# Low halves of stationary weights placed 128 bytes further in their buffer

## The chip, the core and the metric

One core of a Trainium2 chip runs the whole program. The metric is the device time of one execution in microseconds, median of three. In the rows below PE is TensorE's matmuls, PEld its loads of the stationary operand, DVE is VectorE, ACT is ScalarE, POOL is GpSimd, SP the engine that issues the DMAs.

## What is computed

Three transformer layers on 256 tokens of width 1024, in float32: a layer of retention and latent attention, a layer of block attention (MoBA), and a layer of banded attention and a state-space mixer, followed by a feed-forward block of width 4096. Most of the work is products of the activations with large weight matrices:

```
h = x @ w_in                       # per layer, several thousand columns
y = concat([ret_out, mla_out]) @ w_out
h = h + jnp.square(jax.nn.relu(hn @ w_ff1)) @ w_ff2
```

## The kernel before

Every weight matrix comes from HBM in pieces of up to 512 rows by 512 columns, which land in one of three slots of `raw`. ScalarE copies a piece, rounded, into `w_hi` (lines 768 and 778). VectorE, or now and then GpSimd, subtracts that from `raw` and writes the remainder to `w_lo` (line 798). The activations have been split in the same way. A product then takes three matmuls, high by high, high by low and low by high, which add up in PSUM.

There are two layouts. In "tok" chunks (rows of the result are tokens) an activation tile of 128x128 is stationary and 512 columns of weights are moving (lines 1069 to 1071; 1121 to 1123 are a few with 256 moving columns at the end of the program). In "feat" chunks (rows of the result are features) a weight tile of 128x128 is stationary and 256 columns of activations, 1024 bytes on each partition, are moving. Their inner step is this, for each of the four tiles of 128 features in a piece and each 128 rows of weights:

```
pe.matmul(o, wh[k][:, fs], hi[:, ka, :], ...)    # line 1077
pe.matmul(o, wh[k][:, fs], lo[:, ka, :], ...)    # line 1078
ins = pe.matmul(o, wl[k][:, fs], hi[:, ka, :], ...)    # line 1079
```

The stationary tile is loaded anew for each of the three, so that the order of loads is high, high, low, 512 bytes each on every partition. While one matmul runs, the load for the next one runs beside it.

`w_hi` and `w_lo` have two homes each, and a home has two halves of `HALF` = 1024 elements with `SLACK` = 128 elements of spare room behind each. `place(p, e)` turns an element's number in a piece into its place in the buffer. It adds the spare room for the second half, and `p.shift`, which is 80 elements (320 bytes) for pieces of feat chunks and 0 for all others. In the built program the starts of both buffers, of all homes and halves, and of all activation tiles are multiples of 512 bytes. So a feat tile of either part begins 320 bytes past a multiple of 512 bytes, and a moving tile begins on one.

The order of work on each engine is written out by `plan`, and nothing in it depends on `place`. Waits are counted in pieces and half pieces.

Of the kernel before, what the change touches and what calls it, by code (L numbers as in the profile page):

```python
# [7 lines left out]
F32 = mybir.dt.float32  # L8
# [45 lines left out]
HALF = 1024  # L54
SLACK = 128
# [58 lines left out]
class Piece:  # L114


    def __init__(self, chunk, src, nk, k0, cols, order=None, rows=0):
        self.chunk, self.src, self.nk, self.k0, self.cols = chunk, src, nk, k0, cols
        self.order = order
        self.raw = nk * (rows or cols)  # L120
        self.size = nk * cols
        self.turn_after = None
        self.split = False
        self.by_tokens = False
        self.room = 2 * self.size if order == "beside" else self.size
        self.off = 0
        self.shift = 0
        self.home = None
        self.full = nk == 4
        self.ahead_of = None  # L130
# [387 lines left out]
def build(nc, w, out):  # L518
    chunks, pieces, steps = plan(w)
    order = {}  # L520
    for s in steps:
        p = s[1] if s[0] == "piece" else s[1][0] if s[0] in ("part", "rows_of", "tokens") else None
# [17 lines left out]
    for s in steps:  # L540
        if s[0] == "epi":
            c = s[1]
# [4 lines left out]
    with ExitStack() as ctx:  # L547
        def sb(name, shape, dt=F32):
            return ctx.enter_context(nc.sbuf_tensor(name, shape, dt))
# [7 lines left out]
        w_hi = sb("w_hi", [P, 2, 2 * (HALF + SLACK)], F32R)  # L557
# [30 lines left out]
        acc = ctx.enter_context(nc.psum_tensor("acc", [P, 4, 2, 512], F32))  # L588
# [80 lines left out]
                p.home = p.n % 2  # L669

        for p in pieces:
            p.shift = 80 if p.chunk.layout == "feat" else 0

        def room_of(p):

            if p.home == "R3":
                return v_hi[:, :], v_lo[:, :]
            if p.home == "R1":
                return b_hi[:, :], b_lo[:, :]
            return w_hi[:, p.home, :], w_lo[:, p.home, :]  # L680

        def place(p, e):

            if p.home in (0, 1):
                return p.off + e + (p.off + e) // HALF * SLACK + p.shift
            return p.off + e

        def weights_of(p):

            def tiles(b):  # L690
                return [b[:, place(p, k * p.cols):place(p, k * p.cols) + p.cols] for k in range(p.nk)]
            return [tiles(b) for b in room_of(p)]

        def split_views(p, k0, k1):

            r = raw[:, p.slot, k0 * p.raw // p.nk:k1 * p.raw // p.nk]
            at = place(p, k0 * p.cols)
            parts = [b[:, at:at + (k1 - k0) * p.cols] for b in room_of(p)]  # L700
            if p.order == "pairs":
                return [(r.rearrange("p (k f t) -> p k t f", t=2, f=P),
                         *[v.rearrange("p (k t f) -> p k t f", t=2, f=P) for v in parts])]
            if p.order == "beside":
                both = room_of(p)[0][:, at:at + 2 * p.size].rearrange("p (k c n) -> p k c n", k=p.nk, c=2)
                return [(r.rearrange("p (k n) -> p k n", k=p.nk), both[:, :, 0, :], both[:, :, 1, :])]
            if p.order == "twice":
                r = r.rearrange("p (k s) -> p k s", k=p.nk)
                parts = [v.rearrange("p (k c s) -> p k c s", k=p.nk, c=2) for v in parts]
                return [(r, parts[0][:, :, c, :], parts[1][:, :, c, :]) for c in range(2)]  # L710
            return [(r, *parts)]
# [235 lines left out]
        def _(pe):  # L947
# [178 lines left out]
            def rows_of(p, t, k0, k1):  # L1126

                c = p.chunk
                hi, lo = acts[c.acts]
                if p is c.pieces[0] and t == 0:  # L1130
                    before = by_turn[c.turn - 2]
                    pe.wait_ge(*due("acc_read_" + before.reader, before.read_count))
                if c.acts == "cat2":
                    heads_ready(c, p.k0 + k0, p.k0 + k1)
                pe.wait_ge(*due("hi_ready", p.n + 1))
                pe.wait_ge(*due("lo_ready", n_dve[p.n]))
                ts = slice(t * P, (t + 1) * P)
                if p.order == "beside":
                    for h in range(2):
                        for x in (hi, lo):  # L1140
                            for j in range(4):
                                k = 4 * h + j
                                ins = pe.matmul(acc[32 * j:32 * j + 32, c.pair, 0, ts], w_hi[:, p.home, place(p, 0) + 32 * k:place(p, 0) + 32 * k + 32].bitcast(F32), x[:, k, ts].bitcast(F32),
                                                start=(h == 0 and x is hi), stop=(h > 0 and x is lo), skip_group_check=True)
                else:
                    wh, wl = weights_of(p)
                    o = acc[:, c.pair, t, 0:p.cols]
                    for k in range(k0, k1):
                        if c.acts == "x" and k % 2 == 0:
                            pe.wait_ge(*due("mix_hi", 4 * t + k // 2 + 1))  # L1150
                            pe.wait_ge(*due("mix_lo", 4 * t + k // 2 + 1))
                        start, stop = p is c.pieces[0] and k == 0, p is c.pieces[-1] and k == p.nk - 1
                        pe.matmul(o, hi[:, p.k0 + k, ts], wh[k], start=start, stop=False)
                        pe.matmul(o, hi[:, p.k0 + k, ts], wl[k], start=False, stop=False)
                        ins = pe.matmul(o, lo[:, p.k0 + k, ts], wh[k], start=False, stop=stop)
                if t:
                    own(ins, "piece_used")
                elif k1 == p.nk and p is c.pieces[-1] and c.acts == "cat2":
                    own(ins, "mix_used")
# [73 lines left out]
            for _ in range(WARM):  # L1233
                ins = pe.matmul(acc[:, 3, 1, 0:S], gated[:, 0, 0:P], gated[:, 0, :], start=True, stop=True)
            own(ins)
            for s in steps:
# [7 lines left out]
                elif kind == "tokens":  # L1244
                    p, t, k0, k1 = i
# [10 lines left out]
                elif kind == "ret_scores":  # L1256
# [10 lines left out]
                    k = R3[:, 2048:4096].rearrange("p (f s) -> p f s", f=8)  # L1267
                    for j, (o0, i0, n) in enumerate(((0, 0, S), (S, P, P))):
                        for t in range(2):
                            ins = pe.matmul(aux[:, 0, o0:o0 + n], k[:, 2 * h + t, j * P:(j + 1) * P],  # L1270
                                            q[:, 2 * h + t, i0:i0 + n], start=(t == 0), stop=(t == 1))
# [13 lines left out]
                elif kind == "ret_turn":  # L1285
# [5 lines left out]
                    for half in range(2):  # L1291
                        n = 2 * h + half
# [5 lines left out]
                        for f in range(2):  # L1298
                            for t in range(T):
                                c0 = h * RET_DV + (2 * half + f) * P  # L1300
                                ins = pe.transpose(aux[:, 1 - half, f * S + t * P:f * S + (t + 1) * P], gate[:, t, c0:c0 + P], ident)
                        own(ins, "ret_turned")
                elif kind == "scores":
# [28 lines left out]
                    for o0, q0, n in blocks:  # L1332
                        for h in (a, a + 1):
                            r = 64 * (h % 2)
                            o = aux[:, 3 * (h % 2), o0:o0 + n]
                            if a < 8:
                                ins = pe.matmul(o, q_pe[r:r + 64, a // 2, q0:q0 + P], k_pe[r:r + 64, 0, 0:n],
                                                start=False, stop=(o0 > 0), tile_position=(r, 0), skip_group_check=True)
                            elif a < 24:
                                qk = R3[:, :].rearrange("p (q g s) -> p q g s", q=2, g=8)  # L1340
                                ins = pe.matmul(o, qk[r:r + 64, 0, (a - 8) // 2, q0:q0 + P], qk[r:r + 64, 1, (a - 8) // 2, 0:n],  # L1341
                                                start=True, stop=True, tile_position=(r, 0))
                            else:
                                qk = R3[:, 0:2048].rearrange("p (q g s) -> p q g s", q=2, g=4)
                                ins = pe.matmul(o, qk[r:r + 64, 0, (a - 24) // 2, q0:q0 + P], qk[r:r + 64, 1, (a - 24) // 2, 0:n],
                                                start=True, stop=True, tile_position=(r, 0))
                            if o0:
                                own(ins, "scores_ready")
                elif kind == "turn":
# [6 lines left out]
                    for o0, c0 in ((0, 0), (P, P), (2 * P, 2 * P)):  # L1356
                        ins = pe.transpose(aux[:, 1, o0:o0 + P], pr[:, c0:c0 + P], ident)  # L1357
# [16 lines left out]
                elif kind == "values" and i % 2:  # L1374
# [12 lines left out]
                    for t in range(2):  # L1387
                        for h in range(2):
                            o = aux[64 * h:64 * h + 64, 2, (u % 2) * S + t * P:(u % 2 + 1) * S]
                            tp = turned[:, h, 0:S] if t == 0 else turned[:, h, S:3 * P]  # L1390
                            ins = pe.matmul(o, v[:, t, (h0 + h) * DH:(h0 + h + 1) * DH], tp, start=(t == 0), stop=(t == 1), skip_group_check=True)  # L1391
                            if t:
                                ins.then_inc(sems["values_ready"], 1)
                elif kind == "rank_sums":
# [4 lines left out]
                    for r in range(2):  # L1399
                        for t in range(T):  # L1400
                            for k in range(2):
                                ins = pe.matmul(aux[:, 2, 2 * r + t:2 * r + t + 1], sq[:, 2 * r + k, t * P:(t + 1) * P],
                                                ones[:, 0:1], start=(k == 0), stop=(k == 1))
# [5 lines left out]
                elif kind == "dt_sum":  # L1409
                    pe.wait_ge(*due("dt_copied", 1))  # L1410
                    for t in range(T):
                        ins = pe.matmul(acc[:, i.pair, 1, t * SSD_HEADS:(t + 1) * SSD_HEADS], gated[:, 0, t * P:(t + 1) * P], dt_sel[:, :], start=True, stop=True)
# [10 lines left out]
                elif kind == "ssd_cb":  # L1423
# [4 lines left out]
                    for b, (s0, l0) in enumerate(((0, 0), (P, P), (0, P))):  # L1428
                        for g in range(2):
                            n = 2 * b + g  # L1430
                            ins = pe.matmul(aux[:, 2 + n // 4, (n % 4) * P:(n % 4 + 1) * P], b_T[:, g, s0:s0 + P],
                                            c_T[:, g, l0:l0 + P], start=True, stop=True)
                    own(ins, "cb_ready")
                elif kind == "ssd_xs":

                    pe.wait_ge(*due("edge_ready", 1) if i == 0 else due("cb_read", 1))
                    for f in range(8):
                        ins = pe.transpose(aux[:, 2 * i + f // 4, (f % 4) * P:(f % 4 + 1) * P], conv_out[:, f, i * P:(i + 1) * P], ident)
                    own(ins, "xs_turned")
                elif kind == "ssd_rows":  # L1440
# [8 lines left out]
                    for h in range(4):  # L1449
                        for q in range(2):  # L1450
                            r, c = 32 * q, 8 * i + 4 * q + h
# [1062 lines left out]
```

## Time and profile before

| | us |
|---|---|
| median of 3 runs | 793.71 |
| runs | 793.69 to 795.07 |
| the profiled execution | 793.94 |
| its span, first to last instruction | 792.1 |

The profiled execution is 1.8 us longer than its span. In the rows, "mean ns" of a matmul contains its way through the array and is longer than the step from one matmul to the next; the step is read from the starts in the timeline.

### The profile page before, as it was taken

The page shows a single profiled execution, that of the slowest core. Times are in us where ns is not written, and L with a number is a line of the kernel's source. Part 1 is how long each engine was busy: PE and PEld are TensorE (multiplying, and loading weights), DVE is VectorE, ACT ScalarE, POOL GpSimd, SP SyncE. Part 2 cuts the span into 40 slices and gives each one's busy share as a digit, 9 for nine tenths or more (in the row PEclk, how much of TensorE's full clock was granted, in tenths as well). Part 3 has the DMA queues.
Part 4 walks back from the last instruction along what each step waited for, and adds up shares of the span by engine and source line. Part 5 has one row for each costly group of instructions (what it writes and reads, how often), then busy time and mean ns, then how long its engine had stood idle before and what let it go on. Part 6 is the DMA issues. An engine that isn't in the chain of part 4 may idle for free.

```text
span 792.1 us, 13096 instructions
## 1 busy us (share of the span) xinstructions
PE 777.1 (98%) x5084; PEld 684.2 (86%) x5084; DVE 513.4 (65%) x816; ACT 414.8 (52%) x623; POOL 95.5 (12%) x69
## 2 busy tenths in 40 slices
PE   8999999999999999999999899999999999999997
PEld 7998877799988887999787799899777999999996
DVE  6975656666664668468866774886856755555554
ACT  5535445454664553445764667466655544444443
POOL 2331000000100013111300217500000000000002
PEclk9999999999999999999999999999999999999999
DMA  9855643344764644676732464553317565656541
GB/s 332 323 191 183 212 160 109 117 161 114 225 203 158 212 158 132 220 230 193 239 97 75 153 213 142 178 151 117 106 54 219 187 226 194 196 180 207 165 156 53
DMA packets 77051, 137.43 MB, mean 173 GB/s; under 512 B 7104, under 2 KB 15552, under 8 KB 76992
## 3 DMA queue, kind: packets, MB, share of 16 engines
q1 hardware_dynamic: 75744, 132.15, 51.2%
q0 software_dynamic: 1248, 4.46, 1.7%
q8 instruction: 41, 0.67, 0.4%
q14 instruction: 18, 0.15, 0.1%
HBM read 132.80 MB, written 1.05 MB: 169 GB/s over the span
## 4 chain that ended last, share of the span: by engine, by line
PE 89%; DVE 5%; issue 3%; POOL 2%; ACT 1%; DMA 1%; POOLq 0%; ACTq 0%; SPq 0%; DVEq 0%
PE acc L1069 13%; PE acc L1071 13%; PE acc L1070 13%; PE acc L1077 12%; PE acc L1079 12%; PE acc L1078 12%; DVE w_lo L798 2%; PE acc L1357 1%; PE acc L1391 1%; PE acc L1341 1%; PE acc L1330 1%; PE acc L1270 1%; PE acc L1226 1%; DMA raw<-in_w_in_even 1%; PE acc L1452 1%
## 5 line engine op out<-in xcount | busy, mean ns | idle before, releaser
L798 DVE TENSOR_TENSOR w_lo<-raw,w_hi 128x1024 fp32r<-128x1024 f32 (+1 forms) x224 | 274.4, 1241 | 175.0 <-ACT w_hi L778 90.9
L1077 PE MATMUL acc<-x_hi,w_hi 128*128 128x256 f32 x840 | 237.8, 283 | 1.5 <-DVE w_lo L798 1.1
L1079 PE MATMUL acc<-x_hi,w_lo 128*128 128x256 f32 x840 | 235.1, 280 | 0.0
L1078 PE MATMUL acc<-x_lo,w_hi 128*128 128x256 f32 x840 | 235.1, 280 | 0.0
L778 ACT ACTIVATE w_hi<-raw 128x1024 fp32r<-128x1024 f32 (+1 forms) x128 | 133.3, 1043 | 131.3 <-PE acc L1079 68.1
L768 ACT ACTIVATE w_hi<-raw 128x1024 fp32r<-128x1024 f32 x109 | 116.0, 1064 | 113.2 <-PE acc L1079 59.6
L1077 PEld LDWEIGHTS acc<-x_hi,w_hi 128*128 128x128 f32 x840 | 158.1, 188 | 4.9 <-issue 3.1
L1078 PEld LDWEIGHTS acc<-x_lo,w_hi 128*128 128x128 f32 x840 | 159.4, 190 | 0.8 <-issue 0.5
L1079 PEld LDWEIGHTS acc<-x_hi,w_lo 128*128 128x128 f32 x840 | 158.3, 188 | 0.0
L1069 PE MATMUL acc<-w_hi,cat_hi 128*128 128x512 f32 x272 | 109.0, 401 | 0.2 <-DVE w_lo L798 0.2
L1071 PE MATMUL acc<-w_hi,cat_lo 128*128 128x512 f32 x272 | 106.2, 391 | 0.0
L1070 PE MATMUL acc<-w_lo,cat_hi 128*128 128x512 f32 x272 | 106.1, 390 | 0.0
L1069 PE MATMUL acc<-w_hi,x_hi 128*128 128x512 f32 (+1 forms) x192 | 75.9, 395 | 0.0
L1071 PE MATMUL acc<-w_hi,x_lo 128*128 128x512 f32 (+1 forms) x192 | 73.2, 381 | 0.0
L1070 PE MATMUL acc<-w_lo,x_hi 128*128 128x512 f32 (+1 forms) x192 | 73.1, 381 | 0.0
L1069 PEld LDWEIGHTS acc<-w_hi,cat_hi 128*128 128x128 f32 x272 | 51.1, 188 | 12.8 <-issue 3.3
L1071 PEld LDWEIGHTS acc<-w_hi,cat_lo 128*128 128x128 f32 x272 | 51.1, 188 | 11.3
L1070 PEld LDWEIGHTS acc<-w_lo,cat_hi 128*128 128x128 f32 x272 | 51.2, 188 | 9.6
L1069 PEld LDWEIGHTS acc<-w_hi,x_hi 128*128 128x128 f32 x192 | 36.1, 188 | 7.6 <-issue 1.3
L1070 PEld LDWEIGHTS acc<-w_lo,x_hi 128*128 128x128 f32 x192 | 36.2, 188 | 7.4 <-issue 1.0
L1071 PEld LDWEIGHTS acc<-w_hi,x_lo 128*128 128x128 f32 x192 | 36.1, 188 | 7.2
L798 POOL TENSOR_TENSOR w_lo<-raw,w_hi 128x1024 fp32r<-128x1024 f32 (+1 forms) x14 | 31.8, 2291 | 36.5 <-ACT w_hi L768 36.3
(297 smaller groups left out, 912.3 us busy)
## 6 DMA issues: line engine op xcount, KB each, us to landing
raw<-in_w_ff SPq DMA_DIRECT2D x32, 1024.0 KB, 5.2
raw<-in_w_in_even SPq DMA_DIRECT2D x28, 1024.0 KB, 4.9
raw<-in_w_in_odd SPq DMA_DIRECT2D x16, 1024.0 KB, 5.5
raw<-in_w_in SPq DMA_DIRECT2D x16, 1024.0 KB, 5.5
raw<-in_w_out_even SPq DMA_DIRECT2D x12, 1024.0 KB, 5.2
raw<-in_w_out SPq DMA_DIRECT2D x4, 1024.0 KB, 5.2
raw<-in_w_in_even SPq DMA_DIRECT2D x4, 512.0 KB, 6.2
raw<-in_w_ukv_even SPq DMA_DIRECT2D x8, 256.0 KB, 3.2
```

Source lines behind the costliest of these rows:

```text
L768: ins = eng.activation(hi, r, ACT.Copy)
L778: ins = eng.activation(hi, r, ACT.Copy)
L798: ins = eng.tensor_tensor(lo, r, hi.bitcast(F32), ALU.subtract)
L1069: pe.matmul(o, xh, wh[k], start=start, stop=False)
L1070: pe.matmul(o, xh, wl[k], start=False, stop=False)
L1071: ins = pe.matmul(o, xl, wh[k], start=False, stop=stop or (t == 1 and k == p.nk - 1 and p is down[1].pieces[-2]))
L1077: pe.matmul(o, wh[k][:, fs], hi[:, ka, :], start=start and f % 2 == 0, stop=False, skip_group_check=True)
L1078: pe.matmul(o, wh[k][:, fs], lo[:, ka, :], start=False, stop=False, skip_group_check=True)
L1079: ins = pe.matmul(o, wl[k][:, fs], hi[:, ka, :], start=False, stop=stop, skip_group_check=True)
L1226: ins = pe.matmul(aux[:, 2 + g, h * SSD_P:(h + 1) * SSD_P], seg[:, i % 2, h, :], x_dt[:, b, 8 * g + h, :], start=True, stop=True)
L1270: ins = pe.matmul(aux[:, 0, o0:o0 + n], k[:, 2 * h + t, j * P:(j + 1) * P], q[:, 2 * h + t, i0:i0 + n], start=(t == 0), stop=(t == 1))
L1330: pe.matmul(aux[:, 3 * (h % 2), o0:o0 + n], qn[:, q0:q0 + P], kn[:, 0:n], start=(o0 == 0), stop=False, skip_group_check=True)
```

## The change

Pieces of feat chunks get two shifts, 80 elements for the high part as before and 112 elements for the low part. `place` takes the part as a third argument. The low part's 1024 elements of a half end at element 1136 of 1152, so they stay in their half's room. Pieces of tok chunks stay where they were. No instruction is added, removed or moved on any engine: the programs before and after have the same rows in the same order, 4443 on TensorE, 580 on VectorE, 463 on ScalarE, 45 on GpSimd and 47 on SP. The two differ in the addresses at which line 798 writes the low part of feat pieces and the loads for line 1079 read it.

```diff
-            p.shift = 80 if p.chunk.layout == "feat" else 0
+            p.shift = (80, 112) if p.chunk.layout == "feat" else (0, 0)
...
-        def place(p, e):
+        def place(p, e, low):
 
             if p.home in (0, 1):
-                return p.off + e + (p.off + e) // HALF * SLACK + p.shift
+                return p.off + e + (p.off + e) // HALF * SLACK + p.shift[low]
             return p.off + e
...
-            def tiles(b):
-                return [b[:, place(p, k * p.cols):place(p, k * p.cols) + p.cols] for k in range(p.nk)]
-            return [tiles(b) for b in room_of(p)]
+            def tiles(low, b):
+                return [b[:, place(p, k * p.cols, low):place(p, k * p.cols, low) + p.cols] for k in range(p.nk)]
+            return [tiles(low, b) for low, b in enumerate(room_of(p))]
...
-            at = place(p, k0 * p.cols)
-            parts = [b[:, at:at + (k1 - k0) * p.cols] for b in room_of(p)]
+            ats = [place(p, k0 * p.cols, low) for low in range(2)]
+            parts = [b[:, at:at + (k1 - k0) * p.cols] for at, b in zip(ats, room_of(p))]
```

## Rows read from the trace of the kernel before

**Rows 1.** The page: TensorE's busy time, and the chain that ended last, by engine.

```profile
PE 777.1 (98%) x5084; PEld 684.2 (86%) x5084; DVE 513.4 (65%) x816; ACT 414.8 (52%) x623; POOL 95.5 (12%) x69
...
PE 89%; DVE 5%; issue 3%; POOL 2%; ACT 1%; DMA 1%; POOLq 0%; ACTq 0%; SPq 0%; DVEq 0%
```

**Rows 2.** TensorE's groups by line, feat matmuls: count | busy us, mean ns | idle before.

```profile
L1077 PE MATMUL acc<-x_hi,w_hi 128*128 128x256 f32 x840 | 237.8, 283 | 1.5 <-DVE w_lo L798 1.1 <-DVE x_lo L2219 0.4
L1079 PE MATMUL acc<-x_hi,w_lo 128*128 128x256 f32 x840 | 235.1, 280 | 0.0
L1078 PE MATMUL acc<-x_lo,w_hi 128*128 128x256 f32 x840 | 235.1, 280 | 0.0
...
L1079 PE MATMUL acc<-cat_hi,w_lo 128*128 128x256 f32 x40 | 11.0, 276 | 0.0
```

**Rows 3.** Timeline of TensorE, ends of one feat run: start us, length us, instruction.

```profile
686.48 0.39 PE L1071 MATMUL acc<-w_hi,cat_lo 128*128 128x512 f32 x1
686.71 0.28 PE L1077 MATMUL acc<-x_hi,w_hi 128*128 128x256 f32 x1
...
697.90 0.28 PE L1079 MATMUL acc<-x_hi,w_lo 128*128 128x256 f32 x1
698.01 0.40 PE L1069 MATMUL acc<-w_hi,cat_hi 128*128 128x512 f32 x1
```

**Rows 4.** Timeline of TensorE, two matmuls of another feat run, 145 matmuls apart.

```profile
185.00 0.28 PE L1077 MATMUL acc<-x_hi,w_hi 128*128 128x256 f32 x1
...
201.43 0.28 PE L1078 MATMUL acc<-cat_lo,w_hi 128*128 128x256 f32 x1
```

**Rows 5.** Timeline of TensorE, matmuls with tokens on rows and 256 columns, 20 apart.

```profile
784.08 0.28 PE L1121 MATMUL acc<-w_hi,cat_hi 128*128 128x256 f32 x1
...
786.48 0.28 PE L1123 MATMUL acc<-w_hi,cat_lo 128*128 128x256 f32 x1
```

**Rows 6.** Groups by line, 686.7 to 697.9 us, the run of the third group.

```profile
L1077 PE MATMUL acc<-x_hi,w_hi 128*128 128x256 f32 x32 | 9.0, 281 | 0.0
L1079 PE MATMUL acc<-x_hi,w_lo 128*128 128x256 f32 x32 | 9.0, 281 | 0.0
L1078 PE MATMUL acc<-x_lo,w_hi 128*128 128x256 f32 x32 | 9.0, 281 | 0.0
L1078 PEld LDWEIGHTS acc<-x_lo,w_hi 128*128 128x128 f32 x32 | 6.1, 192 | 0.0
L1079 PEld LDWEIGHTS acc<-x_hi,w_lo 128*128 128x128 f32 x32 | 6.0, 188 | 0.0
L1077 PEld LDWEIGHTS acc<-x_hi,w_hi 128*128 128x128 f32 x31 | 5.8, 188 | 0.0
L798 DVE TENSOR_TENSOR w_lo<-raw,w_hi 128x1024 fp32r<-128x1024 f32 x4 | 4.9, 1226 | 6.3 <-ACT w_hi L768 3.3 <-ACT w_hi L778 3.0
```

**Rows 7.** Groups by line, 186 to 201 us, inside the run of the fourth group.

```profile
L1078 PE MATMUL acc<-x_lo,w_hi 128*128 128x256 f32 x39 | 10.8, 276 | 0.0
...
L1078 PEld LDWEIGHTS acc<-x_lo,w_hi 128*128 128x128 f32 x38 | 7.1, 188 | 0.0
L1077 PEld LDWEIGHTS acc<-x_hi,w_hi 128*128 128x128 f32 x38 | 7.1, 188 | 0.0
L1079 PEld LDWEIGHTS acc<-x_hi,w_lo 128*128 128x128 f32 x38 | 7.1, 188 | 0.0
```

**Rows 8.** Groups by line, 784.1 to 786.3 us, inside the run of the fifth group.

```profile
L1122 PE MATMUL acc<-w_lo,cat_hi 128*128 128x256 f32 x7 | 2.0, 283 | 0.0
...
L1121 PEld LDWEIGHTS acc<-w_hi,cat_hi 128*128 128x128 f32 x7 | 1.3, 192 | 0.0
```

**Rows 9.** Line 1078 by stretch: length, PE busy (matmuls) PEld busy (loads), clock, DMA.

```profile
14.30:53.70 39.40, 31.37 (x112) 20.91 (x112) 1.00 0.79 285
...
753.30:764.60 11.30, 8.89 (x32) 6.14 (x32) 1.00 0.61 204
```

**Rows 10.** Groups by line, 700 to 708 us: the split of the next feat pieces.

```profile
L798 DVE TENSOR_TENSOR w_lo<-raw,w_hi 128x1024 fp32r<-128x1024 f32 x4 | 4.8, 1222 | 2.8 <-ACT w_hi L778 1.5 <-ACT w_hi L768 1.3
```

More of the change, by code:

```diff
@@ L126, in __init__ @@
         self.off = 0
-        self.shift = 0
+        self.shift = (0, 0)
         self.home = None
@@ L704, in split_views @@
             if p.order == "beside":
-                both = room_of(p)[0][:, at:at + 2 * p.size].rearrange("p (k c n) -> p k c n", k=p.nk, c=2)
+                both = room_of(p)[0][:, ats[0]:ats[0] + 2 * p.size].rearrange("p (k c n) -> p k c n", k=p.nk, c=2)
                 return [(r.rearrange("p (k n) -> p k n", k=p.nk), both[:, :, 0, :], both[:, :, 1, :])]
@@ L1142, in rows_of @@
                                 k = 4 * h + j
-                                ins = pe.matmul(acc[32 * j:32 * j + 32, c.pair, 0, ts], w_hi[:, p.home, place(p, 0) + 32 * k:place(p, 0) + 32 * k + 32].bitcast(F32), x[:, k, ts].bitcast(F32),
+                                ins = pe.matmul(acc[32 * j:32 * j + 32, c.pair, 0, ts], w_hi[:, p.home, place(p, 0, 0) + 32 * k:place(p, 0, 0) + 32 * k + 32].bitcast(F32), x[:, k, ts].bitcast(F32),
                                                 start=(h == 0 and x is hi), stop=(h > 0 and x is lo), skip_group_check=True)
```

## The prediction

> **What bounds the kernel now.** I read the page first: TensorE's matmuls are busy 98% of the span and make up 89% of the chain that ended last [rows 1]. Whatever lengthens or shortens the step from one matmul to the next reaches the end almost one for one; the other engines matter only through waits, and ahead of the feat matmuls the waits come to 1.5 us in all [rows 2]. Those matmuls, 840 of each line with `x` as the moving operand and 40 more with the ranks, are the ones whose weights the change moves.
>
> Next I read their step, since their mean length is no step. In the run from 686.71 us there are 96 matmuls, so 95 steps from the first to the last, and (697.90 - 686.71) / 95 = 117.8 ns [rows 3]. In another run 145 steps take 201.43 - 185.00 = 16.43 us, which is 113.3 ns [rows 4]. The code, the tile sizes and all places modulo 512 bytes are the same in both. So one stream of instructions has two steady steps, and it keeps the one that it has for dozens of matmuls. A third step stands at the end of the program: matmuls of the same size, but with tokens on rows, where the stationary tile begins on a multiple of 512 bytes just as the moving one does. There 20 steps take 2.40 us, 120.0 ns [rows 5].
>
> The loads tell what these steps have to do with places. At 117.8 ns one load in three takes 192 ns and the others 188, here that of line 1078 [rows 6]. At 113.3 ns all take 188 [rows 7], and at 120.0 ns every one takes 192 [rows 8]. The granted clock is 1.00, its upper level of 2.4 GHz, in the feat stretches [rows 9], so it is not the clock. I read the longer loads as clashes between the stream that loads weights and the stream that reads the moving operand: always where both begin at the same place, one load in three or none where the loads begin 320 bytes further. Per three matmuls the price is 3 x (117.8 - 113.3) = 13.4 ns at the middle step (with the unrounded 117.79 and 113.31), and 3 x (120.0 - 113.3) = 20 ns at the worst.
>
> **How many triples take which step.** A matmul's mean length goes with the step: 281 ns at 117.8 [rows 6], 276 at 113.3 [rows 7]. Over all 840, lines 1078 and 1079 have a mean of 280 [rows 2], so (280 - 276) / (281 - 276) = 80% take the middle step, some 672 triples, with the rounding of the means worth ten per cent either way. From the other side: the eleven long stretches that read 281, from 14.30 to 764.60 us, hold 568 triples (112 in the first, 32 in the last) [rows 9]. I take the middle of the two, 620 at the middle step, and so, with the 40 of the ranks, 880 - 620 = 260 at the best one.
>
> **The change part by part.** Nothing is added, removed or moved, so no engine has another order and no wait is new.
>
> VectorE writes the low part of feat pieces elsewhere. The split of 128x1024 takes 1226 ns where it is for tok pieces, whose parts begin at 0 (the pieces prepared in the feat run), and 1222 ns for feat pieces, whose parts begin 320 bytes further [rows 6, 10]. The place makes no difference that shows: 0 us. One such split serves 8 triples; if each of 880 / 8 = 110 cost 4 ns more, that would be 0.4 us, and VectorE is idle 6.3 us of 11.2 in the run where I looked [rows 6], so that cover would take it.
>
> TensorE's loads for line 1079 read 448 instead of 320 bytes past a multiple of 512. No row shows a load from there. Its cost is bounded by the three steps. Best: every triple takes the 113.3 ns step, 620 x 13.4 = 8.3 us less. Worst: every triple takes the 120.0 ns step, 620 x 3 x (120.0 - 117.8) = 4.1 us and 260 x 20 = 5.2 us, together 9.3 us more.
>
> Between these I take 0, and the reason is a row. At the middle step only one load in three is long, yet the three matmuls of a triple all read 281 ns and not one of them longer [rows 6]. A clash that came once while a 512-byte tile passes, at a point set by where in 512 bytes the tile begins, would fall on one matmul of the three. A delay spread over all three looks like something small that recurs many times inside each tile, so at distances well below 512 bytes. For such a pattern a shift by 128 bytes may be a whole number of repeats: 320 and 448 are both 64 past a multiple of 128, while the tok tiles at 120.0 ns are 0 past one. By this the low loads meet the moving stream as before, at every step.
>
> The Trainium skill speaks against any effect at all: "SBUF — State Buffer", section "Who interferes with whom", gives TensorE two independent read ports, one for the moving operand and one for loads of weights, and says that it never waits on anyone. By that rule the sum is 0 for any shift. The trace does not bear the rule out: it has three steps and two lengths of load for one instruction [rows 6, 7, 8]. So I leave the best and worst ends standing, by the rows.
>
> The page "TensorE: Matmul & The Clock Gate", section "Back-to-back issue gap", gives N / 2.4 + 2.5 ns, so 109.2 ns for 256 columns. Were that within reach, my estimate from that page would be 620 x 3 x 8.6 + 260 x 3 x 4.1 = 19.2 us less. No feat run here shows a steady step under 113.3 ns, and the range does not use it.
>
> The sum: the profiled execution's 793.94 us + 0 (VectorE) + 0 (loads) = 793.94 us. It is 0.23 us above the median of the runs, 793.71; I say 793.8.
>
> **The rivals.**
>
> *The low loads come free of the clash.* For it: one load in three is long, one in three is a low one, and a stream at 113.3 ns keeps it for a hundred matmuls [rows 4, 7]. If the pattern repeats after 512 bytes and not after 128, moving a third of the loads can end the pattern in which each triple pays once. Against it: the long load is that of line 1078 in the run where I looked, a high one [rows 6], and high loads stay where they are. All triples at 113.3 ns: 793.9 - 8.3 = 785.6 us. Half of them, where only some runs come to the better step: 789.8 us.
>
> *The triple loses its even tread.* Now each load begins at the same place modulo 512 bytes as the one before. With the change there are two jumps of 128 bytes in every triple, from high to low and back. If the 113.3 ns step needs equal places, its 260 triples fall to the 117.8 ns step: 260 x 13.4 = 3.5 us, 797.4 us. If the jumps also bring the other 620 to the 120.0 ns step, 4.1 us more, and 5.2 instead of 3.5 for the 260: 803.2 us. It decides as soon as the low loads of the best runs read 192 ns. For it: equal places are all that the 113.3 ns runs have [rows 7]. Against it: high tiles of one piece jump by 512 bytes at every triple without harm.
>
> *The gain is made and not kept.* If TensorE ran 4% faster in feat runs, the next wait would be for pieces: the DMA share is 0.61 to 0.79 there [rows 9], and line 798 has 4.9 us of work in 11.2 [rows 6]. Neither is near its end, so I give this nothing of its own.
>
> **Chances.** Nothing changes: 0.34, and this is the likeliest single case. Faster in all runs (785.6): 0.2. Faster in some (about 789.8): 0.18. Slower by the lost tread, 797.4 or so: 0.18; up to 803.2: 0.1. A measurement of this kernel tells 0.2%, 1.6 us, from no change; so faster 0.38, same 0.34, slower 0.28. The range leaves out the slower tail and little else: 785.3 to 798.5. The likeliest case by itself is 793.2 to 795.1, as the runs of before lie.
>
> **What would show it.** Right: lines 1077 to 1079 again at means of 280 to 283, the run behind the tok chunk at 686 us again at 117.8 ns with one load of 192 ns in each triple, and the runs around 185 us at 113.3. The first rival: that run at 276 ns with all loads at 188. The second: line 1079's loads, or those that follow, at 192 ns in the run around 185 us, and means of 281 or 283 there. What makes me wrong is a pattern that repeats after more than 128 bytes; line 798 slower than 1226 ns would show that VectorE's zero was wrong.

## The result, and the profile after

The changed kernel takes 786.47 us (median of six runs, 785.07 to 787.05), the kernel before 793.7 us (six runs, 792.55 to 795.8). The ratio is 0.9903, with a 95% interval of 0.9893 to 0.9913: 1.0% faster, or 7.2 us. The profiled execution took 786.68 us with a span of 784.9 us, against 793.94 and 792.1 before.

The page of the changed kernel, in the lines that answer to [rows 1]: busy time by engine, and the shares of the chain that ended last.

```profile
PE 770.0 (98%) x5084; PEld 676.7 (86%) x5084; DVE 514.9 (66%) x816; ACT 414.7 (53%) x623; POOL 95.6 (12%) x69
...
PE 89%; DVE 4%; issue 2%; POOL 2%; ACT 1%; DMA 1%; SPq 0%; POOLq 0%; ACTq 0%; DVEq 0%
```

TensorE's matmuls lost 7.1 us of busy time and its loads 7.5 us, and the span is 7.2 us shorter. The number of instructions on each engine is that of [rows 1]. TensorE keeps its 89% of the chain and no other engine's share grew, so nothing took TensorE's place.

TensorE's groups by line for the whole program, as in [rows 2]:

```profile
L1077 PE MATMUL acc<-x_hi,w_hi 128*128 128x256 f32 x840 | 234.9, 280 | 1.2 <-DVE w_lo L798 0.8 <-DVE x_lo L2219 0.4
L1079 PE MATMUL acc<-x_hi,w_lo 128*128 128x256 f32 x840 | 232.2, 276 | 0.0
L1078 PE MATMUL acc<-x_lo,w_hi 128*128 128x256 f32 x840 | 232.1, 276 | 0.0
```

Lines 1078 and 1079 have gone from 280 to 276 ns over all 840, which is what only the best runs had before [rows 7]. The wait ahead of line 1077 is 1.2 us instead of 1.5.

The timeline of TensorE in the run behind the tok chunk, which is the run of [rows 3]. After each start (us) stands the length (us).

```profile
681.08 0.28 PE L1077 MATMUL acc<-x_hi,w_hi 128*128 128x256 f32 x1
681.20 0.28 PE L1078 MATMUL acc<-x_lo,w_hi 128*128 128x256 f32 x1
681.32 0.28 PE L1079 MATMUL acc<-x_hi,w_lo 128*128 128x256 f32 x1
681.44 0.28 PE L1077 MATMUL acc<-x_hi,w_hi 128*128 128x256 f32 x1
681.56 0.28 PE L1078 MATMUL acc<-x_lo,w_hi 128*128 128x256 f32 x1
681.67 0.28 PE L1079 MATMUL acc<-x_hi,w_lo 128*128 128x256 f32 x1
681.78 0.28 PE L1077 MATMUL acc<-x_hi,w_hi 128*128 128x256 f32 x1
...
691.87 0.28 PE L1079 MATMUL acc<-x_hi,w_lo 128*128 128x256 f32 x1
```

The reader is to see a break in the step. The first triple, 681.08 to 681.44 us, takes 0.36 us, which is a slow step of about 120 ns. The second takes 0.34 us, which to the timeline's 0.01 us is the best step already, and the 92 steps from 681.44 to 691.87 us take 10.43 us, 113.4 ns each. So this run still starts slowly, but it comes to the best step after one triple, where before it kept the middle step to its last matmul.

Groups by line inside this run, 681.1 to 691.8 us, as in [rows 6], and the split of feat pieces at 694 to 702 us (last line), as in [rows 10]:

```profile
L1077 PE MATMUL acc<-x_hi,w_hi 128*128 128x256 f32 x32 | 8.8, 276 | 0.0
...
L1078 PEld LDWEIGHTS acc<-x_lo,w_hi 128*128 128x128 f32 x32 | 6.0, 188 | 0.0
L1079 PEld LDWEIGHTS acc<-x_hi,w_lo 128*128 128x128 f32 x32 | 6.0, 188 | 0.0
...
L798 DVE TENSOR_TENSOR w_lo<-raw,w_hi 128x1024 fp32r<-128x1024 f32 x4 | 4.9, 1226 | 6.0 <-ACT w_hi L768 3.1 <-ACT w_hi L778 2.9
```

```profile
L798 DVE TENSOR_TENSOR w_lo<-raw,w_hi 128x1024 fp32r<-128x1024 f32 x4 | 4.8, 1222 | 2.7 <-ACT w_hi L778 1.4 <-ACT w_hi L768 1.3
```

The loads of line 1078 fell from 192 to 188 ns, although they are high parts and did not move. Line 798 takes the same 1226 and 1222 ns as before. Its mean over the whole program rose from 1251 to 1260 ns (128x1024 pieces), but the same kernel run again reads 1254, so no cost of the place is seen. The step of this run is steady although line 798 works for only 4.9 us of it, so its writes do not set the step either.

### The profile page after: what moved, and what is told of

Its sections match the earlier page's. It is cut to its first block, busy times and chain, and to the rows that moved or that the text cites. A ratio compares the mean times of both kernels' runs of the same rounds, so it can differ in the third digit from the quotient of the medians.

```text
span 784.9 us, 13096 instructions
## 1 busy us (share of the span) xinstructions
PE 770.0 (98%) x5084; PEld 676.7 (86%) x5084; DVE 514.9 (66%) x816; ACT 414.7 (53%) x623; POOL 95.6 (12%) x69
## 4 chain that ended last, share of the span: by engine, by line
PE 89%; DVE 4%; issue 2%; POOL 2%; ACT 1%; DMA 1%; SPq 0%; POOLq 0%; ACTq 0%; DVEq 0%
PE acc L1069 13%; PE acc L1071 13%; PE acc L1070 13%; PE acc L1077 12%; PE acc L1079 12%; PE acc L1078 12%; PE acc L1357 1%; DVE w_lo L798 1%; PE acc L1391 1%; DMA raw<-in_w_in_even 1%; PE acc L1341 1%; PE acc L1330 1%; PE acc L1270 1%; PE acc L1226 1%; PE acc L1452 1%
## 5 line engine op out<-in xcount | busy, mean ns | idle before, releaser
L1077 PE MATMUL acc<-x_hi,w_hi 128*128 128x256 f32 x840 | 234.9, 280 | 1.2 <-DVE w_lo L798 0.8
L1079 PE MATMUL acc<-x_hi,w_lo 128*128 128x256 f32 x840 | 232.2, 276 | 0.0
L1078 PE MATMUL acc<-x_lo,w_hi 128*128 128x256 f32 x840 | 232.1, 276 | 0.0
L1078 PEld LDWEIGHTS acc<-x_lo,w_hi 128*128 128x128 f32 x840 | 157.8, 188 | 0.8 <-issue 0.5
```

The lines of the kernel that those rows point to most:

```text
L1077: pe.matmul(o, wh[k][:, fs], hi[:, ka, :], start=start and f % 2 == 0, stop=False, skip_group_check=True)
L1078: pe.matmul(o, wh[k][:, fs], lo[:, ka, :], start=False, stop=False, skip_group_check=True)
L1079: ins = pe.matmul(o, wl[k][:, fs], hi[:, ka, :], start=False, stop=stop, skip_group_check=True)
```

## The experiments

The question is why a shift of the low part alone ends the middle step. Three theories: **place** (bytes 448 past a multiple of 512 are a free place, as the first rival has it), **any jump** (the middle step needs equal places for all three loads, and any difference between high and low ends it), and **repeat** (what counts is the distance from the start of the moving tile to that of the stationary tile, up to whole repeats of some length, and the pair of distances for high and low decides). In what follows a pair such as (64, 192) is these two distances, high and low, in bytes modulo 256. Before, it is (64, 64); after the change, (64, 192).

Each diff is against the changed kernel. Ratios are to the kernel before, run on the same chip: 793.67 us beside the first four, 792.63 beside (16, 48), (16, 80), (80, 96) and the first of the tok pieces, 793.33 beside the others.

**Both parts at 448.**

```diff
-            p.shift = (80, 112) if p.chunk.layout == "feat" else (0, 0)
+            p.shift = (112, 112) if p.chunk.layout == "feat" else (0, 0)
```

> High and low parts both at 112 elements, so the low loads read from the same place as in the changed kernel, and all loads of a triple begin at the same place modulo 512 bytes as in the kernel before. Theory 'place' (448 bytes past a multiple of 512 is out of the way of the moving stream): every feat run at 113.3 ns, all loads 188 ns, about 786.5 us. Theory 'jump' (the unequal places of high and low loads end the pattern in which each triple pays once): the 117.8 ns step is back in most runs, one load in three at 192 ns, about 793.7 us.

Measured: 795.68 us, ratio 1.003 [1.0018, 1.0042]. The timeline of this kernel, first the run behind the tok chunk, then a shorter run:

```profile
688.43 0.28 PE L1077 MATMUL acc<-x_hi,w_hi 128*128 128x256 f32 x1
...
699.62 0.28 PE L1079 MATMUL acc<-x_hi,w_lo 128*128 128x256 f32 x1
```

```profile
535.25 0.28 PE L1078 MATMUL acc<-x_lo,w_hi 128*128 128x256 f32 x1
...
540.46 0.28 PE L1079 MATMUL acc<-x_hi,w_lo 128*128 128x256 f32 x1
```

The first is 95 steps in 11.19 us, 117.8 ns; the second 46 steps in 5.21 us, 113.3 ns. Both steps are back, each kept, with every load at byte 448. The theory of place falls. Groups by line in the first of these runs, 688.4 to 699.6 us:

```profile
L1077 PE MATMUL acc<-x_hi,w_hi 128*128 128x256 f32 x32 | 8.9, 279 | 0.0
...
L1079 PE MATMUL acc<-x_hi,w_lo 128*128 128x256 f32 x31 | 8.7, 280 | 0.0
L1078 PEld LDWEIGHTS acc<-x_lo,w_hi 128*128 128x128 f32 x32 | 6.0, 188 | 0.0
L1079 PEld LDWEIGHTS acc<-x_hi,w_lo 128*128 128x128 f32 x32 | 6.0, 188 | 0.0
L1077 PEld LDWEIGHTS acc<-x_hi,w_hi 128*128 128x128 f32 x31 | 5.8, 187 | 0.0
```

Here the step is 117.8 ns and the loads of all three lines read 187 or 188 ns. So the load of 192 ns, which the prediction took as the mark of a clash, is no sure mark of the lost time. The matmuls read 279 and 280 where the same step read 281 before [rows 6]: at other places the same mean length no longer stands for the same step, so the step itself is what to compare between kernels. The 2 us lost against the kernel before go, at least in part, with runs that had the best step there: the stretch of [rows 4] now takes 16.49 us for 140 steps (184.96 to 201.45), 117.8 ns.

**High and low swapped.**

```diff
-            p.shift = (80, 112) if p.chunk.layout == "feat" else (0, 0)
+            p.shift = (112, 80) if p.chunk.layout == "feat" else (0, 0)
```

> High parts at 112, low parts at 80: the jump has the same size and the other sign, and no low load reads from 448 bytes past a multiple of 512. Theory 'jump': all runs come to 113.3 ns after a few triples, about 786.5 us. Theory 'place of the low load': the low loads are where they were before, so the 117.8 ns step is back, 792 to 794 us; were it any load at 448 that is free, two of three are, and the time lies between.

Measured: 792.41 us, ratio 0.9988 [0.9978, 0.9997]. Timeline, the run behind the tok chunk and the stretch of [rows 4]:

```profile
686.78 0.28 PE L1077 MATMUL acc<-x_hi,w_hi 128*128 128x256 f32 x1
...
697.55 0.28 PE L1079 MATMUL acc<-x_hi,w_lo 128*128 128x256 f32 x1
```

```profile
182.19 0.28 PE L1077 MATMUL acc<-x_hi,w_hi 128*128 128x256 f32 x1
...
200.74 0.28 PE L1077 MATMUL acc<-cat_hi,w_hi 128*128 128x256 f32 x1
```

The first run goes at 10.77 / 95 = 113.4 ns, the second at 18.55 / 156 = 118.9 ns, slower than the old middle step. The jump is as large as in the change, and in the second run it costs. Not every jump will do: it matters which part lies at which distance.

**The low part 128 bytes back instead of on.**

```diff
-            p.shift = (80, 112) if p.chunk.layout == "feat" else (0, 0)
+            p.shift = (80, 48) if p.chunk.layout == "feat" else (0, 0)
```

> High parts at 80, low parts at 48, 128 bytes before the high ones. Theory 'jump': 113.3 ns after a few triples, about 786.5 us. Theory 'place': 192 bytes past a multiple of 512 has no reason to be free, the 117.8 ns step in most runs, about 793.7 us.

Measured: 786.14 us, ratio 0.991 [0.9893, 0.9926], the result of the change. Timeline of the run behind the tok chunk:

```profile
681.16 0.28 PE L1077 MATMUL acc<-x_hi,w_hi 128*128 128x256 f32 x1
...
691.95 0.28 PE L1079 MATMUL acc<-x_hi,w_lo 128*128 128x256 f32 x1
```

95 steps take 10.79 us, as after the change. 192 and 448 are 256 apart, so the pair is (64, 192) again.

**No shift.**

```diff
-            p.shift = (80, 112) if p.chunk.layout == "feat" else (0, 0)
+            p.shift = (0, 0) if p.chunk.layout == "feat" else (0, 0)
```

> No shift: weights and moving tiles all begin on a multiple of 512 bytes, as in the few matmuls with tokens on rows at 120.0 ns. Both theories: every feat run at 120.0 ns with all loads at 192 ns; against the changed kernel some 840 triples x 20 ns = 16.8 us more, about 803 us. If the step of those few matmuls came from their layout and not from the place, it stays at 117.8 or 113.3 ns, 786 to 794 us.

Measured: 801.98 us, ratio 1.0113 [1.0095, 1.0131]. Timeline of the run behind the tok chunk, and TensorE's loads and matmuls in it, 694.3 to 705.7 us:

```profile
694.28 0.28 PE L1077 MATMUL acc<-x_hi,w_hi 128*128 128x256 f32 x1
...
705.67 0.28 PE L1079 MATMUL acc<-x_hi,w_lo 128*128 128x256 f32 x1
```

```profile
L1078 PE MATMUL acc<-x_lo,w_hi 128*128 128x256 f32 x32 | 9.1, 283 | 0.0
...
L1079 PEld LDWEIGHTS acc<-x_hi,w_lo 128*128 128x128 f32 x32 | 6.1, 192 | 0.0
```

95 steps in 11.39 us, 119.9 ns: the third step, which stood at the end of the program before [rows 5], now in feat runs. Of the pairs tried in feat pieces, (0, 0) is the worst.

**The same pair, 256 bytes lower.**

```diff
-            p.shift = (80, 112) if p.chunk.layout == "feat" else (0, 0)
+            p.shift = (16, 48) if p.chunk.layout == "feat" else (0, 0)
```

> High parts at 16 elements, low at 48: 64 and 192 bytes past a multiple of 256, which is what 80 and 112 are too. Theory 'repeat of 256 bytes' (only places modulo 256 bytes count): as the changed kernel, every run at 113.3 ns after a few triples, about 786.4 us. Theory 'repeat of 512 bytes': these are places that no run had, anything from 786 to 802 us.

**High and low 256 bytes apart.**

```diff
-            p.shift = (80, 112) if p.chunk.layout == "feat" else (0, 0)
+            p.shift = (16, 80) if p.chunk.layout == "feat" else (0, 0)
```

> High parts at 16, low at 80: unequal places, 256 bytes apart, both 64 past a multiple of 256. Theory 'repeat of 256 bytes': as the kernel before, most runs at 117.8 ns, about 793.7 us. Theory 'jump' (any inequality of high and low ends the 117.8 ns pattern) or a repeat of 512 bytes: about 786.4 us.

Measured: 786.89 us, ratio 0.9928 [0.9911, 0.9946], for the first; 793.09 us, ratio 1.0004 [0.9993, 1.0014], for the second. Timeline of the run behind the tok chunk, first with (16, 48), then with (16, 80):

```profile
680.99 0.28 PE L1077 MATMUL acc<-x_hi,w_hi 128*128 128x256 f32 x1
...
691.78 0.28 PE L1079 MATMUL acc<-x_hi,w_lo 128*128 128x256 f32 x1
```

```profile
685.25 0.28 PE L1077 MATMUL acc<-x_hi,w_hi 128*128 128x256 f32 x1
...
696.44 0.28 PE L1079 MATMUL acc<-x_hi,w_lo 128*128 128x256 f32 x1
```

10.79 us for 95 steps, as after the change, and 11.19 us, as before it. Moving both parts by 256 bytes leaves the time where it was, and so does moving one of them by 256 bytes. With the change itself, where 128 bytes made 7 us, this fits a repeat of 256 bytes, at the places tried. A jump as such is refuted a second time.

The traces also tell how a run comes by its step where two are open. Of the 31 unbroken runs of 20 or more feat matmuls, 28 take the same step with (16, 80) as in the kernel before. So the step that a run takes is hardly drawn by chance each time; what in its start or ahead of it decides, no experiment here shows. Among the three that differ is the longest: its 328 steps take 38.63 us before (15.01 to 53.64), 117.8 ns, and 37.17 us with (16, 80) (15.08 to 52.25), 113.3 ns. The pair alone therefore doesn't say which of its two steps a run takes. These are counts from one execution of each kernel.

**The low part 64 bytes on.**

```diff
-            p.shift = (80, 112) if p.chunk.layout == "feat" else (0, 0)
+            p.shift = (80, 96) if p.chunk.layout == "feat" else (0, 0)
```

> High parts at 80, low at 96: a jump of 64 bytes instead of 128. Theory 'jump of any size': all runs at 113.3 ns, about 786.4 us. Theory 'high at 64 and low at 192 modulo 256 is the one good pair': steps of 117 to 120 ns in most runs, 793 to 800 us.

Measured: 797.57 us, ratio 1.0069 [1.0047, 1.0091]. Timeline of the run behind the tok chunk:

```profile
693.23 0.28 PE L1077 MATMUL acc<-x_hi,w_hi 128*128 128x256 f32 x1
...
704.47 0.27 PE L1079 MATMUL acc<-x_hi,w_lo 128*128 128x256 f32 x1
```

11.24 / 95 = 118.3 ns. The stretch of [rows 4] takes 16.43 us for 139 steps (184.98 to 201.41), 118.2 ns, so a run that was good before is lost too. So not every distance between the parts brings the gain; (64, 128) is worse than (64, 64).

**Activations moved by 64 bytes, the weights to match.** A spare tile of 64 bytes ahead of `x_hi` and one behind `x_lo` move these two buffers alone, and the shift makes the distances (64, 192) with respect to them. The activations of the ranks (`cat`) stay, so that their pair is (128, 0). Line numbers are two higher in this kernel.

```diff
+        sb("x_gap", [P, 16])
...
+        sb("x_rest", [P, 240])
...
-            p.shift = (80, 112) if p.chunk.layout == "feat" else (0, 0)
+            p.shift = (32, 64) if p.chunk.layout == "feat" else (0, 0)
```

> The activation tiles x_hi and x_lo begin 64 bytes further, and the weights of feat chunks at 32 and 64 elements. Measured from the moving tile, high and low begin at 64 and 192 bytes modulo 256, as in the changed kernel; measured from the start of memory they begin at 128 and 0. Theory 'distance between the two streams': the feat runs on x come to 113.3 ns within a few triples. Theory 'absolute place of the weights': they do not, with steps of 117 to 120 ns. The whole time also moves with the streams that have tokens on rows, whose stationary tiles are shifted too; only the feat step decides.

Measured: 789.73 us, ratio 0.9954 [0.9941, 0.9968]. TensorE's groups by line over the whole program:

```profile
L1080 PE MATMUL acc<-x_lo,w_hi 128*128 128x256 f32 x840 | 232.2, 276 | 0.0
...
L1073 PE MATMUL acc<-w_hi,x_lo 128*128 128x512 f32 (+1 forms) x192 | 74.0, 386 | 0.0
...
L1081 PE MATMUL acc<-cat_hi,w_lo 128*128 128x256 f32 x40 | 11.3, 282 | 0.0
```

Timeline of a run in which the moving operand changes from `x` to the ranks:

```profile
182.48 0.28 PE L1081 MATMUL acc<-x_hi,w_lo 128*128 128x256 f32 x1
...
198.46 0.28 PE L1081 MATMUL acc<-x_hi,w_lo 128*128 128x256 f32 x1
198.58 0.28 PE L1079 MATMUL acc<-cat_hi,w_hi 128*128 128x256 f32 x1
...
205.92 0.28 PE L1081 MATMUL acc<-cat_hi,w_lo 128*128 128x256 f32 x1
```

The 840 triples on `x` keep their 276 ns with both streams elsewhere (95 steps in 10.82 us behind the tok chunk, 683.80 to 694.62), while the 40 on the ranks go from 276 to as much as 282. The run shown has the turn inside one stream: 141 steps on `x` take 15.98 us, 113.3 ns each, and from the first matmul on the ranks, with weights at the same places, 62 steps take 7.34 us, 118.4 ns each. So the weights' own place does not decide, and the distance between the streams fits all runs. That a moving tile 64 bytes past a multiple of 256 is good by itself was not tried with other places of the weights, so that is not ruled out. The total lies 2.9 us above the control below. The tok chunks on `x`, where the moved tile is the stationary one, read 386 ns instead of 381, and 3 x 192 matmuls by 5 ns are 2.9 us; means at different places are no exact price, though, and the ranks lose too.

**Tok pieces moved as well**, to the two shifts of feat pieces (first), both parts to 80 (second) and both to 112 (third); feat pieces as in the change. Here the moving operand shifts.

```diff
-            p.shift = (80, 112) if p.chunk.layout == "feat" else (0, 0)
+            p.shift = (0, 0) if p.order == "beside" else (80, 112)
```

> The changed kernel, and weights that are moving (tokens on rows) shifted by 80 and 112 as well. After each start such a stream of 512 columns takes some 30 ns over nine matmuls more than its steady 226.7 ns a step, in about 55 streams: 1.7 us. If the places set that loss as they set the feat step: 784.5 to 786.4 us. If a shifted moving operand brings the steady step out of its pattern (6 ns on each of some 1400 matmuls): about 795 us. If only the stationary operand's place counts: 786.4 us.

```diff
-            p.shift = (80, 112) if p.chunk.layout == "feat" else (0, 0)
+            p.shift = (80, 112) if p.chunk.layout == "feat" else (0, 0) if p.order == "beside" else (80, 80)
```

> The changed kernel, with high and low weights of chunks with tokens on rows, which are moving there, both at 80 elements. The run with 80 and 112 there lost the steady 226.7 ns step to one of 230 ns. If the inequality of two moving tiles did that, the step is 226.7 ns again, and the settling after each start, some 30 ns in 55 streams, is shorter or longer by up to 1.7 us: 784.8 to 788 us. If any shift of the moving tile does it: about 789.5 us as there.

```diff
-            p.shift = (80, 112) if p.chunk.layout == "feat" else (0, 0)
+            p.shift = (80, 112) if p.chunk.layout == "feat" else (0, 0) if p.order == "beside" else (112, 112)
```

> The same with both at 112 elements, 192 bytes modulo 256 in place of 64. If only the inequality of the two moving tiles cost time: 784.8 to 788 us, and 226.7 ns steps. If the distance to the stationary tile counts as it does in feat chunks, this one and the one at 80 differ in their settling by up to 1.7 us.

Measured: 789.46 us, ratio 0.996 [0.9946, 0.9974]; 788.77 us, 0.994 [0.9918, 0.9961]; 793.6 us, 1.0002 [0.9988, 1.0016]. All three keep the 276 ns of lines 1078 and 1079. The first and the third are slower than the change; the second lies 2.0 us above the control below, and their intervals overlap. Timeline of a tok chunk with 512 moving columns, in the changed kernel and then in the third of these:

```profile
648.37 0.40 PE L1069 MATMUL acc<-w_hi,cat_hi 128*128 128x512 f32 x1
...
659.05 0.39 PE L1071 MATMUL acc<-w_hi,cat_lo 128*128 128x512 f32 x1
```

```profile
653.22 0.39 PE L1069 MATMUL acc<-w_hi,cat_hi 128*128 128x512 f32 x1
...
664.18 0.39 PE L1071 MATMUL acc<-w_hi,cat_lo 128*128 128x512 f32 x1
```

47 steps in 10.68 us, 227.2 ns, against 10.96 us, 233.2 ns; the same chunk takes 10.84 us, 230.6 ns, with the first edit and 10.76 us, 228.9 ns, with the second. For 512 columns, both streams at a multiple of 512 bytes is the best place tried, by this chunk. For the 256 columns at the end of the program it is not, as the changed kernel and then the second of these show:

```profile
776.47 0.28 PE L1121 MATMUL acc<-w_hi,cat_hi 128*128 128x256 f32 x1
...
779.22 0.28 PE L1123 MATMUL acc<-w_hi,cat_lo 128*128 128x256 f32 x1
```

```profile
777.61 0.28 PE L1121 MATMUL acc<-w_hi,cat_hi 128*128 128x256 f32 x1
...
780.22 0.28 PE L1123 MATMUL acc<-w_hi,cat_lo 128*128 128x256 f32 x1
```

23 steps in 2.75 us, 119.6 ns, fall to 2.61 us, 113.5 ns. That gains 0.14 us in this run.

**The changed kernel again**, beside the last three, as a control.

> The changed kernel as it is, on the same chip as the two that shift the moving weights, to compare them with it: about 786.4 us, 0.99 of the kernel before.

Measured: 786.8 us, ratio 0.9919 [0.9897, 0.9941]. No version tried is faster than the changed kernel by more than the intervals; those with the pair (64, 192) and nothing else moved are its equals.

The feat placements together, in steps of the runs read above, those of the first pair without the slow start. Where two steps stand, some runs take the one and some the other.

| pair modulo 256 | shifts | steps, ns | median, us |
|---|---|---|---|
| (64, 192) | 80/112, 80/48, 16/48 | 113.4 | 786.47, 786.14, 786.89 |
| (192, 64) | 112/80 | 113.4 and 118.9 | 792.41 |
| (64, 64) | 80/80, 16/80 | 113.3 and 117.8 | 793.7, 793.09 |
| (192, 192) | 112/112 | 113.3 and 117.8 | 795.68 |
| (64, 128) | 80/96 | 118.3 | 797.57 |
| (0, 0) | 0/0 | 119.9 | 801.98 |

## Why the prediction was wrong

**What bounds the kernel: right.** It said that the step of the feat matmuls reaches the end almost one for one. The 7.1 us less of matmul time made 7.2 us less of span, and the 8.3 us more without any shift (801.98 against 793.67) came through the same steps.

**The failed step** is the one that chose 0 between the two ends for TensorE's loads: "A delay spread over all three looks like something small that recurs many times inside each tile, so at distances well below 512 bytes. For such a pattern a shift by 128 bytes may be a whole number of repeats". By it the loads' term of the sum was 0; measured, it is about 7.2 us less. The even 281 ns of the three matmuls [rows 6] was a true reading, but the repeat drawn from it was half as long as the one that the runs show. Two places 256 bytes apart behave alike (16/48 as 80/112, 16/80 as 80/80), and two places 128 bytes apart do not. That 320 and 448 are both 64 past a multiple of 128 was therefore no reason for 0. One row could not decide between 128 and 256, and the prediction said that a pattern repeating after more than 128 bytes would make it wrong; it is so.

**The reading of the loads** failed too. Long loads were called clashes and the mark of the lost time. With both parts at 448 the step of 117.8 ns stands with every line's loads at a mean of 187 or 188 ns, so load length and step go together only at some places.

**The rival that came true** is the low loads that come free, at 785.6 us against 786.47 measured. It was right that the pattern repeats after more than 128 bytes and that moving a third of the loads can end it. But the low loads do not come free by where they lie: byte 448 is not free in itself (both at 448: 795.68 us). What the change ends is that a slow step keeps itself: in the trace of the changed kernel a run begins with a few slow triples, or with none, and then goes at the best step. In the pairs with equal distances, (64, 64) and (192, 192), either step was kept once a run had settled, within a triple or two; with (64, 192) only the better one was. This much the timelines show; the reason for it they don't.

**The price was nearly right.** 620 triples by 13.4 ns gave 8.3 us at the best end; 7.2 us were measured. In the run at 681 us the saving is 11.19 - 10.79 = 0.40 us, where 32 triples by 13.4 ns make 0.43, and most of the difference is the slow start, whose first two triples take 0.70 us where the best step makes 0.68. Over the program such starts take a part of the missing 1.1 us; since the runs of the changed kernel alone lie 2.0 us apart, I don't divide it further.

**The rival on the lost tread** did not happen with this pair, but was no idle one: (64, 128) and, in the stretch of [rows 4], (192, 64) took the good run to 118.2 and 118.9 ns. Its worst end, 120.0 ns in every run for 803.2 us, was near to what no shift at all brought, 801.98; but no shift has no jump, so that confirms the price and not the mechanism. A jump of 256 bytes (16, 80) cost nothing.

**VectorE at 0 us: right**, by the unchanged 1226 and 1222 ns of line 798. **A gain made and not kept: right to give it nothing**, since the wait ahead of line 1077 fell from 1.5 to 1.2 us.

**The rule weighed against the row.** The prediction doubted what the Trainium skill says in "SBUF — State Buffer", section "Who interferes with whom", that TensorE waits on nobody and its two read ports are independent. By that rule all these placements would take one time. They have the same instructions and lie between 786.14 and 801.98 us, so here the measurement decides against it. The prediction doubted the rule and still came to the same 0 by another way.

What stays open: why the distance counts modulo 256 bytes, why (64, 192) brings every run to the best step and (192, 64) only some, and what in its start sets the step that a run takes where two keep themselves.

## What to carry to other kernels

When one stream of matmuls shows two steps start to start with the same code and the same clock, try where the stationary tiles begin against the moving ones, for each load of the pattern by itself and at several places within 256 bytes; here that was worth 15.8 us between the worst placement and the best, without an instruction more. That 256 bytes is the repeat elsewhere too, for other types or shapes, is not shown. Decide by steps and not by mean lengths, and look at how a run begins as well as how it goes on. Tune each tile size by itself and look at all users of a buffer that moves: what was worst for 256 columns was best for 512.

## What was unexpected in the hardware

- The step of one matmul (128x128 stationary, 256 moving columns) took values from 113.3 to 119.9 ns at the same granted clock, 1.00 in the stretches read, and which values it can take went with the distance of its two operands modulo 256 bytes. For 512 columns it ran from 227.2 to 233.2 ns.
- A stream keeps a step for dozens of matmuls once it has it: 117.8 and 113.3 ns stand in one program with equal places, in [rows 3] and [rows 4] and with both parts at 448. Which of the two a run takes is largely the same from kernel to kernel, 28 runs of 31 for the pair (64, 64).
- The order of the distances matters: (64, 192) gives 786.47 us, (192, 64) gives 792.41.
- A load of 192 instead of 188 ns is no measure of the time lost: 117.8 ns came with the loads of one line in three at a mean of 192 ns, and with none.
